# Filler products in the last pair of experts, and ScalarE's copy of the transposed probabilities moved within a softmax step

## The reference

```
for i in range(DEPTH):                       # DEPTH = 2
    mix = moba_attention(x, ...) if i % 2 == 0 else nsa_attention(x, ...)
    x = layer_norm(DEEPNORM_ALPHA * x + mix, ln_g[i, 0], ln_b[i, 0])
    ffn = grouped_moe(x, router_w, router_b, w_gate[i], w_up[i], w_down[i])
    x = layer_norm(DEEPNORM_ALPHA * x + ffn, ln_g[i, 1], ln_b[i, 1])
```

```
hid = silu(xt @ w_gate[e]) * (xt @ w_up[e])  # 1024 x 512 each
return hid @ w_down[e]                       # 512 x 1024
```

## Time and profile before

| | us |
|---|---|
| median of three runs | 1193.33 |
| the profiled execution | 1195.33 |
| its span, first to last instruction | 1193.5 |
| PE busy | 1014.6 (85%) |
| DVE busy | 356.2 (30%) |
| ACT busy | 184.5 (15%) |
| DMA, mean rate over the span | 376 GB/s |

### The profile page before, as it was taken

How to read it: one execution, slowest core, us unless ns; L and a number is a source line. 1 busy time by engine, 2 the same in 40 slices (tenths; PEclk the granted TensorE clock), 3 DMA queues, 4 the chain that set the end, 5 groups by cost and what they waited for, 6 DMA issues and landing times.

```text
span 1193.5 us, 18920 instructions
## 1 busy us (share of the span) xinstructions
PE 1014.6 (85%) x7872; PEld 565.5 (47%) x7872; DVE 356.2 (30%) x888; ACT 184.5 (15%) x474; POOL 55.7 (5%) x133
## 2 busy tenths in 40 slices
PE   9999999976698966678899999999866898766765
PEld 7595544543343533344599655444533434423432
DVE  4745612221111111111567775213111111111112
ACT  1023211100010100000321663111100000000001
POOL 1012010000000000000100230100000000000000
PEclk9999999987799987789999999999977899878898
DMA  9937899999999999999992719999999999999994
GB/s 352 373 142 288 343 394 419 426 427 429 427 427 427 428 427 428 428 424 423 371 362 84 283 35 364 391 418 427 427 427 426 428 427 427 427 427 427 427 423 191
DMA packets 59351, 449.12 MB, mean 376 GB/s; under 512 B 4579, under 2 KB 10980, under 8 KB 32636
## 3 DMA queue, kind: packets, MB, share of 16 engines
q1 hardware_dynamic: 57248, 442.52, 90.2%
q0 software_dynamic: 1680, 4.88, 1.2%
q10 hardware_dynamic: 332, 0.42, 0.1%
HBM read 446.72 MB, written 1.07 MB: 375 GB/s over the span
## 4 chain that ended last, share of the span: by engine, by line
PE 55%; DMA 40%; DVE 2%; ACT 1%; issue 1%; SPq 1%; DVEq 0%
PE bank L1220 15%; DMA ring<-in_moe_w_up 14%; DMA ring<-in_moe_w_down 11%; DMA ring<-in_moe_w_gate 10%; PE bank L1001 7%; PE bank L1184 5%; PE bank L1072 5%; DMA bias<-in_moe_w_up 5%; PE bank L1305 3%; PE bank L1281 2%; PE bank L1469 2%; PE bank L1320 2%; PE bank L1041 1%; PE bank L1292 1%; PE bank L1496 1%; PE bank L1063 1%
## 5 line engine op out<-in xcount | busy, mean ns | idle before, releaser
L1220 PE MATMUL bank<-ring,work 128*32 128x256 f32 (+1 forms) x2656 | 336.4, 493 | 106.9 <-DMA ring<-in_moe_w_gate 35.5
L1220 PEld LDWEIGHTS bank<-ring,work 128*32 128x32 f32 (+1 forms) x2656 | 154.5, 136 | 244.4 <-issue 217.2
L1950 DVE TENSOR_TENSOR work<-work,bank 128x256 f32<-128x256 f32 (+1 forms) x32 | 15.6, 488 | 520.6 <-PE bank L1220 520.6
L1305 PE MATMUL bank<-ring,work 128*32 128x512 f32 x576 | 91.9, 627 | 11.6 <-DMA ring<-in_moe_w_down 7.2
L1220 PE MATMUL bank<-softmax_area,work 128*32 128x256 f32 (+1 forms) x352 | 65.8, 503 | 33.8 <-DMA ring<-in_moe_w_gate 25.4
L1963 DVE TENSOR_TENSOR xs<-xs,bank 128x512 f32<-128x512 f32 x112 | 71.1, 684 | 41.8 <-PE bank L1323 23.6
L1220 PE MATMUL bank<-bias,work 128*32 128x256 f32 (+1 forms) x384 | 78.1, 499 | 0.0
L1184 PE MATMUL bank<-work,acc 128*128 128x128 f32 (+1 forms) x448 | 75.5, 323 | 0.0
L1184 PEld LDWEIGHTS bank<-work,acc 128*128 128x128 f32 x448 | 66.0, 191 | 16.6 <-issue 11.5
L1220 PEld LDWEIGHTS bank<-softmax_area,work 128*32 128x32 f32 (+1 forms) x352 | 31.9, 141 | 66.6 <-issue 60.9
L2388 ACT COPY work<-bank 128x256 f32<-128x256 f32 (+1 forms) x32 | 13.6, 425 | 319.4 <-PE bank L1257 252.3
(11 more groups left out here) (331 smaller groups left out, 1273.9 us busy)
## 6 DMA issues: line engine op xcount, KB each, us to landing
ring<-in_moe_w_gate SPq DMA_DIRECT2D x44, 2048.0 KB, 29.2
ring<-in_moe_w_up SPq DMA_DIRECT2D x40, 2048.0 KB, 28.6
ring<-in_moe_w_down SPq DMA_DIRECT2D x36, 2048.0 KB, 29.2
softmax_area<-in_moe_w_down SPq DMA_DIRECT2D x8, 2048.0 KB, 25.1
ring<-in_moe_w_down SPq DMA_DIRECT2D x12, 1024.0 KB, 8.4
ring<-in_moe_w_gate SPq DMA_DIRECT2D x12, 1024.0 KB, 9.3
bias<-in_moe_w_gate SPq DMA_DIRECT2D x6, 2048.0 KB, 34.6
softmax_area<-in_moe_w_up SPq DMA_DIRECT2D x6, 2048.0 KB, 27.7
```

The source lines that it names most:

```text
L1220: last = mm(bank[2 + k][row:row + cap, 0:width], xgT_of(group_of[i])[:, t, at + e * cap:at + (e + 1) * cap], w[e](t)[:, part * width:(part ...
L1305: last = mm(bank[5][row:row + CAP_NARROW, :], hidT_narrow[:, m, CAP_NARROW * e:CAP_NARROW * (e + 1)], w[e](m)[:, n * 512:(n + 1) * 512], s ...
```

## The change

There are two parts. In the last pair of each layer, TensorE issues three filler products of 512 columns into bank 2 ahead of the gate block, behind its wait for the reading of that bank, and four instead of one into bank 3 ahead of the up block. And on ScalarE the copy of the transposed probabilities becomes a function; in a step s of 2 or more with nothing beside it the copy of job s - 2 is issued ahead of the exponentials of step s, in all others behind them as before.

```diff
                 if "gate" in blocks:
                     pe.wait_ge(silu_ready, PAIRS * l + i)
+                    if i == PAIRS - 1:
+                        keep_warm(3, b=2)
                     block(0, range(KT)).then_inc(gate_done, 1)
...
                 if i == PAIRS - 1:
                     acc_to_psum(l)
-                    keep_warm(1, b=3)
+                    keep_warm(4, b=3)
                 block(1, range(KT)).then_inc(up_done, 1)
...
             def softmax_steps(l):
 
+                def copy_probsT(j):
+                    act.wait_ge(probsT_ready[l], j + 1)
+                    after(act, pv_done[l], j - 1)
+                    s_.copy(probsT[:, 2 * (j % 2) + 1, :], bank[5][:, 0:3 * P]).then_inc(probsT_act, 1)
+
                 n_steps = len(job_pairs[l])
                 for s in range(n_steps + 2):
...
+                    unfilled = not beside[l].get(s)
+                    if s >= 2 and unfilled:
+                        copy_probsT(s - 2)
                     if s < n_steps:
                         act.wait_ge(scores_read[l], s + 1)
...
-                    if s >= 2:
-                        j = s - 2
-                        act.wait_ge(probsT_ready[l], j + 1)
-                        after(act, pv_done[l], j - 1)
-                        s_.copy(probsT[:, 2 * (j % 2) + 1, :], bank[5][:, 0:3 * P]).then_inc(probsT_act, 1)
+                    if s >= 2 and not unfilled:
+                        copy_probsT(s - 2)
```

## The result

The changed kernel took 1197.19 us (median of 20 runs, 1195.41 to 1199.25), the kernel before in the same comparison 1193.28 (20 runs); the ratio is 1.0034, 95% interval 1.0028 to 1.0041. It is slower, by about 3.9 us; 1192.3 was forecast, with 1189.8 to 1196.0 as the range. The profiled execution took 1197.52 us, its span 1195.7 (before 1195.33 and 1193.5). So the two profiles are only 2.2 us apart: the profiled execution of the kernel before is 2.05 above its median, that of the changed kernel 0.33.

The account below looks back on a forecast made before the run. The experts were taken to end when their weights have arrived, with loads following the attention's end. 1195.33 - 0.95 (copies) - 0.96 (layer 1's fillers) = 1193.42; from the median, 1193.33 - 0.95 = 1192.38, forecast 1192.3, range 1189.8 to 1196.0.

Parts of the forecast that it names:

- The copies: Layer 1's attention, softmax step 5: TensorE's wait for ScalarE's copy goes; -0.95 us, bounds -1.19 and +4.1.
- late next: Softmax step 5: GpSimd's scaling (to 674.75) and VectorE's half of the copy (to 674.80) next hold up the transposes.
- The rival that blocks ScalarE: Softmax steps: all nine moved copies make their exponentials late by 0.46 us, 1197.5 us; chance 0.10.
- The fillers in layer 0: Last pair: the added products cost 0, hidden by the 1.67 us wait for down weights; bounds 0 and +0.99.
- fillers to 552.44 + 2.66 = 555.10: Layer 0's last pair: three fillers of 2.66 us start when TensorE runs out of work at 552.44.
- The fillers in layer 1: Last pair: up block ends 1.54 us earlier, down weights' landing limits the gain; -0.96 us, bounds -1.54 and +0.15.
- this case (1192.38): Layer 1's last pair: runs near the median had no slow up block, so fillers give nothing; 1193.33 - 0.95 = 1192.38.
- Code loading: Rival: the 0.96 us stop in pair 14's up block moves into the last pair, giving 1193.3 us; chance 0.05.
- the stop stands in pair 14, not in what ends last: Argument against a stop for code in the last pair: the trace shows it in pair 14 in both layers.
- signs of being wrong: VectorE idle until exponentials in unfilled steps; last pair's gate or up block above 5 us, or an uncaused stop there.
- signs of being right: Step 5's copy wait gone, step 7 0.95 earlier; layer 1's up block 3.7 us, then idle; layer 0's end unmoved.

Follow-up runs that it names:

- the code moved back: Changed kernel with 58 products in layer 0 and 52 in layer 1 added to the branch that is not taken; 1193.05 us, ratio 1.0000.
- the copies alone: Kernel before with only the softmax copies moved, the extra products left out; 1192.30 us against 1193.19, ratio 0.9994.
- the shift alone: Kernel before with 6 products in layer 0 and 12 in layer 1 added to the branch that is not taken; 1194.24 us, ratio 1.0007.
- the kernel before at the new place: Kernel before with 18 products in layer 0 and 12 in layer 1 added to the branch that is not taken; 1192.59 us, ratio 0.9992.
- the boundary is at row 4: Changed kernel with 6 products in layer 0 and 62 in layer 1 added to the branch that is not taken; 1198.89 us, ratio 1.0038.
- the changed kernel at the new place: Changed kernel with 12 products in layer 0 added to the branch that is not taken; 1191.70 us, ratio 0.9987.

## Why the prediction was wrong

- *The copies.* Right in the trace: -0.95 forecast, 0.83 measured; in the time of the whole kernel the runs don't settle it. GpSimd and VectorE were named as late next, and it is VectorE. Its copy ends at 677.41 and TensorE starts 0.26 later; 0.14 had been taken, from ScalarE's copy, and that is the difference. The rival that blocks ScalarE did not happen: step 5's exponentials come 0.34 later, where 0.26 had been worked out, and cost nothing.
- *The fillers in layer 0*, forecast at 0 with a bound of +0.99, cost 2.61 with the late pair 14. The step that failed is "fillers to 552.44 + 2.66 = 555.10": it took the end of pair 14's work, 552.44, as given. In the changed kernel it is 555.82, and the wait of 2.59 that was to pay for the fillers no longer exists. The sum of the rest was sound: with the code moved back they lie in the waits.
- *The fillers in layer 1*, forecast at -0.96, failed at the same step: TensorE was free from 1156.75 in the working, from 1160.48 in the run. The gain was most likely not there to be had either: the slow up block is in the one profiled execution of before. With the copies alone, with the shift alone and with the kernel before at the new place the last up block takes 3.66 us in layer 1 without any added filler; the forecast's sum named this case (1192.38) and leaned to it.
- *Code loading* was the right mechanism with the wrong place and price. It was given 0.05, and a stop of 0.96 that would have to move into the last pair. It had only to move within pair 14, by 12 and 36 rows, which could be counted from the diff and the two copies of `last_pairs`. The size was off as well: stops of 2.45 and 2.24 us, then 48 and 52 rows with the clock at or near 0.50, some 3 to 3.6 us a layer. And "the stop stands in pair 14, not in what ends last" holds only while the last pair has idle time to give; the same idle time had been spent on the fillers.
- *The signs.* None of the prediction's signs of being wrong showed, since those for the experts looked inside the last pair. Two of its signs of being right failed: the end of layer 0 came 2.61 late, and no idle time stands ahead of layer 1's last products.
- *What the stop waits for.* The moved kernels fit boundaries every 256 instructions, or a divisor of that. The Trainium skill, "Advanced Engine Details and Errata", ISA Cache, gives 256 instructions for a line, and the trace agrees as far as that goes. The trace also shows code arriving: an instruction transfer runs in 537 to 538 us in layer 0 of the kernel before and of the changed kernel, and in the next microsecond where the boundary is at row 4, each time 1 to 3 us after the block's first product. In all 14 stops of the kernels above TensorE goes on 2.5 to 2.9 us after the beginning of the half microsecond in which this transfer is listed. That fits a stop which the transfer ends, though no run moved the transfer alone, and it fits the lengths: after row 28 the stop is 0.80 us in the kernel before (transfer at 537.0) and 2.04 with the copies alone (transfer at 539.0). The transfer runs as well where no stop stands in the block (537.5 in the changed kernel at the new place). A second page bears on the place behind the branch: the Trainium skill, "Runtime: NRT & Kernel Launch", Instruction fetch mechanics, says that the engine fetches the next page while it executes the current one, and that a taken branch breaks this. The trace agrees in so far as these stops stand in the first code behind the branch, with such a transfer ahead of the restart. This is the row of the changed kernel's DMA queues from 537 to 538 us (packets, MB, share):

```profile
q8 instruction: 1, 0.02, 6.6%
```

What stays open is how the 2.5 us between transfer and restart divide; and that the transfer is late because the DMA engines are full of weights (shares of 0.99 to 1.03 in the stretches above) was not tried.

## What to carry to other kernels

Code that is added ahead of a branch target, in a branch that never runs too, moves what stands behind it against the boundaries at which code is fetched: count the instructions, find the stop called "issue" behind the branch in the trace, and work out after which row it will stand. Idle time can hide one thing only: before two costs are put down as hidden, add them up against the same wait. A few instructions that are never executed are then a cheap knob: here they turned a loss of 0.34% into a gain of 0.13%, against the kernel before, for the same work.

## What the runs showed of the hardware

- The stop's place in the program is fixed (after 28 rows in layer 0 of three kernels, 16 in four), but its length isn't: 0.52, 0.80 and 2.04 us for the same place, and after row 47 of layer 1 it shows in one of three. It ended 3.9 to 5.5 us after the block's first product, whether 4 or 47 rows had run, and 2.5 to 2.9 us after the beginning of the half microsecond with the instruction transfer. That transfer in turn follows the one before it by 5.5 to 6.5 us, in both layers of all twelve kernels.
- A stop of 2.45 us after 16 rows left TensorE at 0.50 for the 5 us that followed; one of 0.80 after 28 rows was followed by 1.00. The place is not all that counts: one of 2.04 after 28 rows, with the copies alone, was followed by 0.93 for 1.2 us and then by 0.50.
- Against the new place, where no stop stands in the block, the changed kernel's blocks are 4.57 and 4.14 us longer (9.67 - 5.10, 10.02 - 5.88). Of that 2.45 and 2.24 are the stops, and about as much is rows that run slower.
